# First mixer loop of a hybrid decoder trunk: six of each head's twelve products as split fp32r products

## What is computed

```
def _mix(h, l, prm, past):
    proj = h @ prm['w_in'][l]
    hq, hf, hi, hg, sq, sk, sv, mx, mo, ga, gb, gc = jnp.split(proj, _in_split_points(), axis=-1)
    ...
    o_a, S_new = _hgrn2(hq, hf, hi, hg, lb, S0, prm['hg_gain'][l], hg_chunk)
    ...
    o_b = _sb_attend(q, jnp.concatenate([pk.astype(k.dtype), k], axis=1), ...)
    ...
    o_c, (C_new, n_new, m_new, buf_new) = _mlstm(mx, mo, buf0, l, prm, C0, n0, m0, ml_chunk)
    merged = (jax.nn.sigmoid(ga.astype(f32)) * (o_a @ prm['w_hg_proj'][l])
              + jax.nn.sigmoid(gb.astype(f32)) * (o_b @ prm['w_sb_proj'][l])
              + jax.nn.sigmoid(gc.astype(f32)) * (o_c @ prm['w_ml_proj'][l]))
    y = (merged @ prm['w_out'][l]).astype(h.dtype)
```

## Time and profile before

| | |
|---|---|
| median of 3 runs | 1940.47 us (1938.87 to 1941.92) |
| the profiled execution | 1941.34 us |
| its span, first to last instruction | 1939.6 us |
| TensorE busy / weight loads busy | 1806.4 us (93%) / 1544.9 us (80%) |
| VectorE / ScalarE busy | 965.1 us (50%) / 721.7 us (37%) |
| granted TensorE clock, mean | 0.968 of full speed |
| DMA, mean over the span | 202 GB/s |

### The profile page before, as it was taken

How to read it: one execution, slowest core, us unless ns; L and a number is a source line. 1 busy time by engine, 2 the same in 40 slices (tenths; PEclk the granted TensorE clock), 3 DMA queues, 4 the chain that set the end, 5 groups by cost and what they waited for, 6 DMA issues and landing times. The chain is left out here.

```text
span 1939.6 us, 32975 instructions
## 1 busy us (share of the span) xinstructions
PE 1806.4 (93%) x12392; PEld 1544.9 (80%) x12392; DVE 965.1 (50%) x1739; ACT 721.7 (37%) x1317; POOL 80.4 (4%) x111
## 2 busy tenths in 40 slices
PE   6999989999999997999959999899999999979997
PEld 4998967777876786998959889778777767869997
DVE  3555333364367635654355554343453665266554
ACT  3554333133233204654345553232233221056542
POOL 0000010000001001000010000100000000010001
PEclk7999989999999998999979999899999989989998
DMA  8678633652547832556537777425633587325661
GB/s 329 252 297 321 243 129 121 250 200 78 222 153 274 285 109 87 178 201 262 228 147 278 283 290 270 165 79 217 244 118 137 177 311 246 109 92 188 213 237 52
DMA packets 85923, 391.50 MB, mean 202 GB/s; under 512 B 12472, under 2 KB 17856, under 8 KB 55488
## 3 DMA queue, kind: packets, MB, share of 16 engines
q1 hardware_dynamic: 72816, 368.24, 51.2%
q10 hardware_dynamic: 13008, 21.94, 3.1%
HBM read 377.32 MB, written 12.83 MB: 201 GB/s over the span
## 5 line engine op out<-in xcount | busy, mean ns | idle before, releaser
L1001 DVE TENSOR_TENSOR ring_parts<-ring,pages_parts 128x1024 fp32r<-128x1024 f32 (+1 forms) x272 | 314.5, 1191 | 200.7 <-ACT pages_parts L1561 200.6
L469 PE MATMUL ps<-xn,ring 128*128 128x264 f32 x1664 | 386.3, 392 | 6.0 <-ACT xn L1568 6.0
L508 PE MATMUL ps<-arena_parts,pages_parts 128*128 128x264 f32 x1408 | 362.6, 292 | 23.2 <-DVE xn_parts L1069 21.6
L469 PEld LDWEIGHTS ps<-xn,ring 128*128 128x128 f32 x1664 | 317.8, 193 | 65.3 <-issue 8.5
L509 PE MATMUL ps<-xn_parts,pages_parts 128*128 128x264 f32 x1408 | 357.2, 288 | 0.0
L1561 ACT ACTIVATE pages_parts<-ring 128x1024 fp32r<-128x1024 f32 (+1 forms) x272 | 267.9, 1025 | 181.4 <-DMA ring<-in_w_ffn_in 71.2
L508 PEld LDWEIGHTS ps<-arena_parts,pages_parts 128*128 128x128 f32 x1408 | 271.6, 193 | 43.9 <-issue 43.2
L509 PEld LDWEIGHTS ps<-xn_parts,pages_parts 128*128 128x128 f32 x1408 | 271.0, 192 | 0.0
L513 PE MATMUL ps<-arena_parts,ring_parts 128*128 128x264 f32 x1408 | 196.6, 283 | 0.0
L508 PE MATMUL ps<-big_parts,pages_parts 128*128 128x264 f32 x704 | 177.8, 288 | 6.6 <-DVE gates_parts L1015 6.6
L513 PEld LDWEIGHTS ps<-arena_parts,ring_parts 128*128 128x128 f32 x1408 | 180.7, 188 | 0.0
(11 more groups left out here) (312 smaller groups left out, 2052.2 us busy)
## 6 DMA issues: line engine op xcount, KB each, us to landing
ring<-in_w_ffn_in SPq DMA_DIRECT2D x88, 1024.0 KB, 4.9
ring<-in_w_ada SPq DMA_DIRECT2D x32, 1536.0 KB, 6.7
ring<-in_w_a SPq DMA_DIRECT2D x32, 1536.0 KB, 11.6
ring<-in_w_ffn_down SPq DMA_DIRECT2D x32, 1408.0 KB, 6.2
pages<-in_k_pages SPq DMA_DIRECT2D x128, 256.0 KB, 5.4
pages<-in_v_pages SPq DMA_DIRECT2D x128, 256.0 KB, 4.0
ring<-in_w_ada SPq DMA_DIRECT2D x24, 1024.0 KB, 7.3
ring<-in_w_proj SPq DMA_DIRECT2D x8, 1536.0 KB, 9.2
```

Of the source, the lines that this page charges most:

```text
L469: last = mm(ps[:, b, 0:T], tile_of(r, first + k), rhs(k), start=(k == 0), stop=(k == depth - 1))
L508: mm(ps[:, b, 0:T], tile, hi[:, k, :], start=start, stop=False)
L1001: v.tensor_tensor(ring_lo[:, r, at * P:(at + n) * P], w, whi[:, place, 0:n * P].bitcast(F32), ALU.subtract)\
```

## The change

In the A loop the six products of slots 1 and 2 become split fp32r products. The others of the head (slots 3 and 4) and w_sq stay float32. Because xn is still needed, the split input gets new places: the high part in `gates` 16 to 23, the low part in the ring slot that the loop no longer uses. The loop runs on three ring slots: loads 1 and 3 of a head share one. The high weights are staged in halves of 4 tiles (512 columns) with four places: two in `oc` (big 20 to 23), one behind the low input in the free slot, one in `ft`. The halves of a head's first two products are split at the end of the head before (the first head's before the w_sq evacuations), those of the third at the head's start, those of products 4 to 6 on ScalarE behind the evacuations of products 1 to 3. The loop over heads is written out on TensorE, VectorE and ScalarE (POOL keeps its `Fori`). SP issues loads 1 and 2 of the next head ahead of the second page group. `first_ffn_slot` of the second FFN and `split_input` only get other counts.

```diff
+HALF = KC // 2
+A_SLOTS, A_FREE = (1, 2, 1, 3), 0
+A_ORDER = ((0, 1, 2), (2, 0, 1))
...
+        return [(self.pos + j) % SLOTS for j in A_SLOTS], (self.pos + A_FREE) % SLOTS
...
+        xhi_a = gate_parts[:, 2 * KC:3 * KC, :]
+        def free_slot(r):
+            spare = ring_lo[:, r, :]
+            return spare[:, 0:KC * T].rearrange("p (c t) -> p c t", c=KC), spare[:, KC * T:KC * T + HALF * P]
...
 # SP
+                at, _ = slots.places()
+                for k in range(2):
+                    load(ins.w_a[layer, k], 3, at[k])
+                sp.wait_ge(S.yss_ready, 1)
                 for i in range(HEADS):
-                    for k in range(3):
-                        load(ins.w_a[layer, i * 4 + k], 3)
-                    sp.wait_ge(S.yss_ready, 1)
+                    load(ins.w_a[layer, i * 4 + 2], 3, at[2])
                     load_key_pages(i * 2)
-                    load(ins.w_a[layer, i * 4 + 3], 3)
+                    load(ins.w_a[layer, i * 4 + 3], 3, at[3])
+                    if i < HEADS - 1:
+                        for k in range(2):
+                            load(ins.w_a[layer, i * 4 + 4 + k], 3, at[k])
                     load_key_pages(i * 2 + 1)
+                sp.wait_ge(S.tr, HEADS)
...
 # TensorE
+                def halved_product(r, first):
+                    b, n = products.take()
+                    pe.wait_ge(S.evac, n + 1)
+                    for h in range(2):
+                        place, m = pieces.take()
+                        pe.wait_ge(S.wlo_ready, m + 1)
+                        for k in range(h * HALF, (h + 1) * HALF):
+                            tile = hi_halves[place][:, k % HALF * P:(k % HALF + 1) * P]
+                            mm(ps[:, b, 0:T], tile, xhi_a[:, k, :], start=(k == 0), stop=False)
+                            last = mm(ps[:, b, 0:T], tile, xlo_a[:, k, :], start=False, stop=False)
+                        last.then_inc(S.whi_done, 1)
+                        for k in range(h * HALF, (h + 1) * HALF):
+                            last = lower(b, r, first + k, k, xhi_a, k == KC - 1)
+                    last.then_inc(slot_done[r], 1)
...
-                        for k in range(2):
-                            r = open_slot(3)
-                            for n in ((0, 1, 2), (2, 0, 1))[k]:
-                                product(r, n * KC, xn_of, KC)
+                    for k in range(2):
+                        r = open_slot(3, at[k])
+                        for n in A_ORDER[k]:
+                            halved_product(r, n * KC)
...
 # VectorE
+                def split_halves(r, first):
+                    for h in range(2):
+                        place, m = pieces.take()
+                        tiles = slice((first + h * HALF) * P, (first + (h + 1) * HALF) * P)
+                        dve.wait_ge(S.whi_ready, m + 1)
+                        v.tensor_tensor(ring_lo[:, r, tiles], ring[:, r, tiles], hi_halves[place].bitcast(F32),
+                                        ALU.subtract).then_inc(S.wlo_ready, 1)
+                split_input(2, xhi_a, xlo_a)
+                for n in range(2):
+                    split_halves(at[0], A_ORDER[0][n] * KC)
...
+                for i in range(HEADS):
...
+                    split_halves(at[0], A_ORDER[0][2] * KC)
+                    for n in range(3):
+                        split_halves(at[1], A_ORDER[1][n] * KC)
...
                     v.tensor_copy(kdt[:], ps[:, M0, 0:TP].rearrange("p (t q) -> p t q", t=2)).then_inc(S.kdtr, 1)
+                    if i < HEADS - 1:
+                        for n in range(2):
+                            split_halves(at[0], A_ORDER[0][n] * KC)
...
 # ScalarE
+                def split_halves(slot, first):
+                    r, loads, _ = slot
+                    act.wait_ge(slot_full[r], loads * 16 + 16)
+                    for h in range(2):
+                        place, m = pieces.take()
+                        act.wait_ge(S.whi_done, m + 1)
+                        A(hi_halves[place], ring[:, r, (first + h * HALF) * P:(first + (h + 1) * HALF) * P], ACT.Copy)\
+                            .then_inc(S.whi_ready, 1)
...
+                for i in range(HEADS):
+                    split_halves(w_slot, A_ORDER[0][2] * KC)
...
                     for k in range(2):
-                        r, _, before = slots.take(3)
+                        r, _, before = slots.take(3, at[k])
                         for n in range(3):
-                            evac(r, before + 2 + n, dests[3 * k + n])
+                            if k == 0:
+                                evac(r, before + 2 + n, dests[n])
+                                split_halves(w_slot, A_ORDER[1][n] * KC)
+                            else:
+                                evac(r, before + 2 + n, dests[3 + n])
...
                     evac(r, before + 3, gates[:, i * 4 + 2, :], exp=True)
+                    if i < HEADS - 1:
+                        w_slot = ahead.take(3, at[0])
+                        for n in range(2):
+                            split_halves(w_slot, A_ORDER[0][n] * KC)
                     act.wait_ge(S.ho, i + 1)
```

More of the change, by code:

```diff
@@ L107, in take, with places @@
         return r, self.loads[r](), self.parts[r](parts)
+    def places(self):
+        return [(self.pos + j) % SLOTS for j in A_SLOTS], (self.pos + A_FREE) % SLOTS
     def follow(self, other):
@@ L195, in build @@
         fe = sb("fe", [P, 2, T])
-        ft = sb("ft", [P, 2, T])
+        ft, ft_parts = twins("ft", [P, 2, T])
         big, big_parts = twins("big", [P, 28, T])
@@ new lines, in _ @@
+                at, free = slots.places()
+                xlo_a, hi_halves = free_slot(free)[0], halves_of(free)
+                def halved_product(r, first):
[12 more added lines that the diff above has]
+                    last.then_inc(slot_done[r], 1)
@@ L1144, in _ @@
                 modulate_samples(1)
-                split_input(1)
+                split_input(1, xhi, xlo)
                 split(2 * KC)
@@ L1201, in _ @@
                 before_a = products.count.n
-                with dve.Fori(0, HEADS) as i, slots.loop(i, HEADS, [3] * 4), products.count.loop(i, HEADS, 12), \
-                        link.loop(i, HEADS, 22):
+                for i in range(HEADS):
                     for k in range(4):
-                        slots.take(3)
+                        slots.take(3, at[k])
                         for n in range(3):
                             products.take()
+                    split_halves(at[0], A_ORDER[0][2] * KC)
+                    for n in range(3):
+                        split_halves(at[1], A_ORDER[1][n] * KC)
                     link(v.tensor_copy(lbh[:], lbt[:, bds(layer * HEADS + i, 1), :].rearrange("p a b -> p (a b)")))
@@ L1676, in evac @@
                     A(dst, ps[:, b, 0:T], ACT.Exp if exp else ACT.Copy, scale=-1.0 if exp else 1.0).then_inc(S.evac, 1)
+                ahead.follow(slots)
+                for s in range(2):
+                    ahead.take(2)
+                at, free = ahead.places()
+                hi_halves = halves_of(free)
+                def split_halves(slot, first):
+                    r, loads, _ = slot
+                    act.wait_ge(slot_full[r], loads * 16 + 16)
+                    for h in range(2):
+                        place, m = pieces.take()
[5 more added lines that the diff above has]
+                    split_halves(w_slot, A_ORDER[0][n] * KC)
                 for s in range(2):
@@ L1695, in _ @@
                 before_a = products.count.n
-                with act.Fori(0, HEADS) as i, slots.loop(i, HEADS, [3] * 4), products.count.loop(i, HEADS, 12), \
-                        link.loop(i, HEADS, 14):
+                for i in range(HEADS):
+                    split_halves(w_slot, A_ORDER[0][2] * KC)
                     act.wait_ge(S.dve_it, i + 1)
@@ L1716, in _ @@
                     softplus_tail(sbt, zp).then_inc(S.lnr, 1)
-                    r, _, before = slots.take(3)
+                    r, _, before = slots.take(3, at[2])
                     evac(r, before + 2, dests[6])
@@ L1740, in _ @@
                     last.then_inc(S.qkv_sb, 1)
-                    r, _, before = slots.take(3)
+                    r, _, before = slots.take(3, at[3])
                     act.wait_ge(S.dlr, i + 1)
```

202 lines of the change are left out of this document (103 added, 99 removed).

## The result

The changed kernel takes **1914.47 us** (median of 4 runs, 1901.47 to 1915.84) against 1939.79 us (median of 4) for the kernel before on the same chip: ratio 0.9851, 95% interval 0.9831 to 0.9871. The forecast was 1908.7 us, range 1899 to 1924. The gain is 25.3 us instead of 31.8. The profiled execution took 1915.48 us, and its span is 26.2 us shorter than the one in the earlier trace rows.

A forecast was written before the change was run, and what follows sets the result against it. TensorE, busy 93% of the span, was taken to bound the kernel. 1941.3 - 29.8 (products) - 2.0 (heads written out) = 1909.5 us for the profiled execution, 1908.7 against the median; range 1899 to 1924.

The forecast's parts named there:

- The case forecast as the likeliest: Whole kernel: 1903 to 1916 us, varying with the clock, third-product stalls and written-out heads; chance 70%.
- Products: Six products per head on TensorE: 2.94 instead of 3.56 us each, 48 products, gain 29.8 us.
- (a): Head's end: four halves split ahead on ScalarE and VectorE during waits, cost 0; without cover 2.8 us a head.
- (b): Third product's split at the head's start: cost 0, bound 0 to 0.6 us a head.
- (c): Products four to six, split behind earlier products' evacuations: margin 3.4 us, cost 0.
- (d): Head loop's start: VectorE makes the high and low input, covered by four w_sq products, 14.2 us; cost 0.
- Ring and queues: Three slots and SP's new order: load 3 has 8.8 us, nearest row 8.1; page waits unchanged; cost 0.
- the partial transfer wait of 15%: Load 3 or the second page group makes TensorE wait 1 to 3 us a head: 1917 to 1933 us; chance 15%.
- Heads written out: Shorter gaps between ScalarE's DMA issues before VectorE's L1241: 0.25 us a head, 2.0 us in all.
- The clock: Half-clock stretch on TensorE, seen from the third head, may come or go by 1.5 us; 3 us allowed either way.
- The rival on weight loads: 24 weight loads for 16 bound TensorE: 5.34 us a product, 85 us more, 2026 us; chance 1%.

The follow-up runs named there:

- the pair with wide columns: Changed kernel with 128-column sample matmuls, 1903.78 us, against the same with all products f32 and no splits, 1932.94 us.
- e10_wide_no_split_ahead: Changed kernel with 128-column sample matmuls, heads 2 to 4 splitting their first two products at their own start: 1934.16 us, ratio 0.9953.
- e3_three_slots_f32: Changed kernel with all products in f32 and no splits; three slots, new SP order and written-out heads kept: 1940.97 us, ratio 0.9999.
- e8_wide_pages_first: Changed kernel with 128-column sample matmuls, second page group issued ahead of the next head's loads 1 and 2: 1915.01 us, ratio 0.9859.
- e4_unrolled_before: Kernel before with only its head loop written out on TensorE, VectorE and ScalarE; four slots, f32: 1938.42 us, ratio 0.9992.
- the pairs: Split against all-f32 products, three slots: with 128-column sample matmuls 1903.78 against 1932.94 us, with one column 1914.8 against 1940.97 us.
- e1_again: The changed kernel measured again with no edit: 1914.8 us, ratio 0.9859.

## Why the prediction came out as it did

The case forecast as the likeliest is the one that happened, with 6.5 us less gain than its sum.

- **Products, -29.8 us.** Right: 2.93 us each, and -29.2 us in the pair with wide columns. The FFN pieces were the right row to price from. The page "FP8 and Floating Point Precision" of the Trainium skill (TensorE Precision Notes) states four passes for true FP32; that reduced FP32 takes one is the prediction's reading of it. The estimate from these was 2.67 us per product; the trace has 2.93, and the measurement decides.
- **(a) splits ahead, cost 0.** Right: VectorE ends them at 352.02, and L1369 (L1304 before) follows at 352.10, without a wait of TensorE. The price without cover, 2.8 us a head, was right for the wait (2.92) and too low for the whole: e10_wide_no_split_ahead lost 30.4 us, not the 6 x 2.8 = 17 of the six heads that have one before them, with stretches of low clock worth about 10 us behind the waits. That an uncovered wait is followed by lost clock was missing from the price.
- **(b) third product, 0 of 0 to 0.6.** Right: halves split by 364.5 on ScalarE and 365.2 on VectorE, wanted at 367.05.
- **(c) margin of 3.4 us.** Right: the fourth product's first half is copied at 365.35, VectorE's part ends at 366.70, and it is wanted at 369.97: 3.3 us. **(d)** no wait in the trace.
- **Ring and queues, 0.** Right: load 3 landed after 6.2 us where 8.1 was the nearest row; key pages 4.8 us in all against 5.6. e3_three_slots_f32 agrees within its 3 us, with 1940.97 us. Its rival, the partial transfer wait of 15%, did not happen, but e8_wide_pages_first shows that another order on SP makes it real, by way of the splits on ScalarE and VectorE: 11 us.
- **Heads written out, -2.0 us.** In the right direction, and too large. The wait it was to shorten fell by 8.2 - 6.9 = 1.3 us, and by 1.2 in e4_unrolled_before, where nothing else was changed; as times, e3_three_slots_f32 shows 0 and e4_unrolled_before -1.5 us, both within the noise.
- **The clock, 3 us either way.** This is the term that was mis-sized, as "such a stretch may come or go". It was read as a coin toss in one head. The two traces of the changed kernel have four and six stretches of 3.4 us behind the block of narrow matmuls (L819), the kernel before one. By the pairs this cost the change 3.0 us (1.7 by the ratios), which is not clear of the noise. The granted clock of all executions points to more: its mean over an execution was 0.9696 in the 23 executions of the kernel before beside e1_again and 0.9647 in the six of e1_again. That is 59 and 68 us of missing clock over the span, up to 9 us more, of which only the part counts in which TensorE was what the rest waited for. So it was a loss where the sum had 0; whether it stayed within the 3 us allowed is not shown. As a whole the narrow matmuls cost the changed kernel about 11.0 us by the medians.

So of the missing 6.5 us about 0.7 is the written-out heads' smaller gain and 2 to 3 are clock by the pairs; by the granted clock it may be all the rest, and the spread of 1901 to 1919 us is wider than what is to be explained. No run here divides it further. It is also luck that the median lies in the forecast case, near its upper end: the clock's loss depends on where the stretches fall, and single executions of the changed kernel lie on both sides of 1903 to 1916 us.

The rival on weight loads (2026 us) did not happen either: PEld's share rose from 80% to 81% and TensorE's time fell by 29.1 us, with products at 2.93 us instead of 5.34. The page "Perfetto Trace Analysis" of the Trainium skill (Identifying the Most-Contended Engine) judges TensorE's headroom by the LDWEIGHTS busy share; 80% and 81% tell nothing of those 29.1 us.

## What to carry to other kernels

Price a new kind of instruction from a place in the same kernel that already runs it back to back: 2.94 us forecast, 2.93 measured. When work is taken off the bounding engine, look at the granted clock at the same places after the change, since a stretch in which the matmuls stand 0.21 instead of 0.12 us apart hides in "busy" time. When helpers prepare operands ahead, the price of losing that cover can be more than the wait: here 17.5 us of waits came with about 10 us of lost clock.

## What was not expected

- Low-clock stretches of 3.4 us stand behind eight matmuls of one column (L819, 16 passes of 250 ns, TensorE recorded as busy). Streaming 128 columns costs 275 ns a pass and 1.95 instead of 1.84 us a block. The five traces with narrow products have 14 such stretches behind the 40 blocks. The seven with wide ones have none, unless TensorE also stood idle there: e8_wide_pages_first has one after a wait of 1.86 us inside the block, e10_wide_no_split_ahead five after its waits. The wide columns are worth 11.0 us in the changed kernel, 8.0 with three slots and f32, and 1.5 (unclear) in the kernel before.
- These three gains go with the clock. The mean granted clock over all executions rose from 0.9647 to 0.9714 in the changed kernel (13 us of its span), from 0.9676 to 0.9713 with three slots and f32 (7 us) and from 0.9703 to 0.9715 in the kernel before (2 us). Why the clock is lost so unequally was not settled. The matmuls ahead of the block are the same in all of them. The heads begin at other times in each, and they do so between executions of one kernel too, but no run isolated that.
- Executions of one code spread by 17 us (1901.47 to 1918.68 for the changed kernel, ten runs), where the wide version's five stayed within 4.4 us. That the clock makes the whole of the difference in spread was not shown: the wide f32 kernel spread over 11 us.
